# Spreading the gates of a product-key layer: one product moved from VectorE to GpSimd, masks and casts in another layout

## The chip, the core and the metric

The kernel runs on one core of a Trainium2 chip. The core has five engines with their own instruction streams: TensorE (PE in the rows; PEld is its weight load), VectorE (DVE), ScalarE (ACT), GpSimd (POOL) and SyncE (SP, which here issues DMAs only). They share the on-chip memory SBUF; TensorE writes to PSUM. Engines wait for one another through semaphores. The metric is the device time of one execution in microseconds (us); less is better.

## What is computed

One step of a one-layer encoder over 1024 prompt frames and 64 frames of a running stream: a normalised projection, band attention and retention side by side, and then PEER, a retrieval over 128 x 128 single-neuron experts. Only PEER matters here:

```
s = einsum('thcd,hckd->thck', qry, sub_keys)         # 8 heads, 2 halves, 128 keys each
top_s, top_i = top_k(s, 16)                          # per half
cand_s = top_s[..., 0, :, None] + top_s[..., 1, None, :]
cand_i = top_i[..., 0, :, None] * 128 + top_i[..., 1, None, :]
best_s, best_pos = top_k(cand_s, 16)                 # 16 of the 256 pairs
expert = take_along_axis(cand_i, best_pos)
gate = softmax(best_s)
a = einsum('td,thkd->thk', h, expert_u[expert])
y = einsum('thk,thkd->td', gelu(a) * gate, expert_v[expert])
```

A token so has 8 x 16 = 128 slots, each with a first place i and a second place j (both 0 to 127) and a gate. For 640 of the tokens the kernel does not gather rows but multiplies by all 16384 experts, with a gate matrix G[i, j] per token that is zero but at the chosen pairs. Building this matrix is the job of the spread stage:

G[i, j] = sum over slots s of (i == place_i[s]) * (j == place_j[s]) * gate[s]

## The kernel before

The program is a row of stages with a barrier of all engines behind each: `project`, `mix` (attention and retention, out projection), `route` (the two top-k searches), `spread`, `experts`. A stage is a block in which each engine has its own function; the order on an engine is the order in which its function is written, and nothing else sets it.

`spread` takes 5 tiles of 128 tokens (`NTD`), each in 16 steps of `B` = 8 tokens: 80 steps. The 128 slots lie on the 128 partitions. In a step

- VectorE (L1616) forms `hot_j`: for each of the 8 tokens a row of 128 places that is 1 where the place is the slot's j. Its layout is [slot, token, place], so its second operand, the slot's j, is constant along the innermost axis (a broadcast with step 0).
- VectorE (L1620) forms `hot_i` likewise for i, but in the layout [slot, place, token]: innermost are the 8 tokens, whose i values lie side by side, and the broadcast is over the middle axis.
- VectorE (L1625) multiplies `hot_j` by the gate (again a broadcast along the innermost axis): `cols`, in f32.
- ScalarE (L1658) casts `hot_i` to f32 `rows` and turns it to [slot, token, place] on the way, reading every eighth element.
- TensorE (L1641) multiplies, for each of the 8 tokens, `rows` (128 x 128) by `cols` (128 x 128) into PSUM `gp`; a multiplication has two entries in the trace, so a step has 16.
- ScalarE (L1662) copies `gp` into the tile's matrix `g`, turned to [i, j, token]. It does so one step late: cast of step q, then copy of step q - 1. At the end of a tile it makes the last copy before the next tile's first cast.

`hot_i`, `hot_j`, `rows` and `cols` have two buffers each, `gp` has four. The waits are: `hot_i` of a step needs the cast of two steps earlier; `cols` and the cast need the multiplication of two steps earlier; the multiplication needs both `rows` and `cols`. In the trace `g` is called `spr_g` for even tiles and `pass_g` for odd ones. A tile's matrix is stored by SyncE with one DMA, the last one in four pieces by ScalarE (L1674), and the `experts` stage starts on these.

The rows ahead of the spread stage come from other stages: `mix` uses GpSimd for squares (L585), rotary products (L602, L603, L605) and the product with a decay that is constant along the innermost axis (L615); `route` uses it for a product of bf16 tiles (L1183); `experts` for the low halves of weights (L1799). VectorE's neighbours there are L757 and L763 (two scalings of queries and keys), and L1391 in `route`.

## Time and profile before

| | us |
|---|---|
| median of 3 runs | 3593.18 (3587.45 to 3594.58) |
| time of the profiled execution | 3587.85 |
| its span in the trace | 3586.1 |
| spread stage: first VectorE step to the issue of the last stores | 1465.35 to 1710.62 |
| VectorE busy between 1465 and 1711 us | 230.45 |
| ScalarE busy there | 230.00 |
| TensorE busy there | 170.54 |
| GpSimd busy there | 0.00 |

Times in the rows are counted from the start of the span. A timeline row is "start, duration, engine, line, operation, output<-inputs, shapes, x count", and in brackets the idle time of the engine before it with what ended it. A row with x2 or more is several instructions put together, and its duration runs from the first start to the last end. Instructions of one engine may overlap by a tenth of a microsecond: the next starts while the former drains, so the spacing of starts, not the duration, is what a step costs. The engine "PEq" in a bracket is TensorE's queue, here the barrier between two stages.

### The profile page before, as it was taken

The page shows a single profiled execution, that of the slowest core. Times are in us where ns is not written, and L with a number is a line of the kernel's source. Part 1 is how long each engine was busy: PE and PEld are TensorE (multiplying, and loading weights), DVE is VectorE, ACT ScalarE, POOL GpSimd, SP SyncE. Part 2 cuts the span into 40 slices and gives each one's busy share as a digit, 9 for nine tenths or more (in the row PEclk, how much of TensorE's full clock was granted, in tenths as well). Part 3 has the DMA queues.
Part 4 walks back from the last instruction along what each step waited for, and adds up shares of the span by engine and source line. Part 5 has one row for each costly group of instructions (what it writes and reads, how often), then busy time and mean ns, then how long its engine had stood idle before and what let it go on. Part 6 is the DMA issues. An engine that isn't in the chain of part 4 may idle for free.

```text
span 3586.1 us, 51512 instructions
## 1 busy us (share of the span) xinstructions
PE 3311.0 (92%) x18470; PEld 2838.7 (79%) x18470; DVE 2502.0 (70%) x5310; ACT 1080.2 (30%) x1689; POOL 1762.7 (49%) x1341
## 2 busy tenths in 40 slices
PE   8999996999988997477799999999999999999999
PEld 6888885566656997466698998998888888888887
DVE  3111103434332999899388999999999899999998
ACT  3111112334331221699322222222222222222221
POOL 0000004332300365000477887888887788788786
PEclk9999997999999999799899999999999999999999
DMA  4222215222232000157899999999999899999998
GB/s 174 100 91 99 99 61 201 81 96 91 95 126 84 16 22 15 36 167 226 268 335 334 376 365 353 375 358 359 385 372 350 330 359 363 352 365 355 366 372 303
DMA packets 338482, 831.47 MB, mean 232 GB/s; under 512 B 25904, under 2 KB 132784, under 8 KB 336048
## 3 DMA queue, kind: packets, MB, share of 16 engines
q0 software_dynamic: 129024, 469.82, 34.9%
q1 hardware_dynamic: 165456, 314.88, 25.0%
q10 hardware_dynamic: 43872, 45.29, 3.7%
q8 instruction: 51, 0.84, 0.1%
q14 instruction: 79, 0.65, 0.1%
HBM read 741.09 MB, written 88.80 MB: 231 GB/s over the span
## 4 chain that ended last, share of the span: by engine, by line
PE 35%; DVE 11%; issue 2%; POOL 2%; DMA 2%; ACT 0%; DVEq 0%; ACTq 0%
PE exp_up L2055 17%; PE exp_vp L2072 17%; DVE exp_now L2001 6%; DMA pass_g<-in_u_rows,pass_g 2%; DVE pass_g L1972 1%; DVE exp_ring L1994 1%; DVE pass_g L1994 1%; DVE exp_up L1958 1%; POOL exp_v_lo L1804 1%; POOL exp_u_lo L1799 1%; POOL pass_g L1813 1%; DVE exp_am_lo L1963 0%; POOL exp_ring L1813 0%; DMA exp_ring<-in_u_rows,pass_g 0%; DVE exp_now L1997 0%
## 5 line engine op out<-in xcount | busy, mean ns | idle before, releaser
L2055 PE MATMUL exp_up<-dense_h_hi,exp_u_hi 128*128 128x320 f32 x2048 | 647.5, 316 | 54.6 <-DVE exp_am_lo L1963 30.1
L2055 PE MATMUL exp_up<-dense_h_lo,exp_u_hi 128*128 128x320 f32 x2048 | 634.2, 310 | 0.0
L2055 PE MATMUL exp_up<-dense_h_hi,exp_u_lo 128*128 128x320 f32 x2048 | 632.5, 309 | 0.0
L1972 DVE TENSOR_TENSOR pass_g<-pass_g,exp_vp 128x512 f32<-128x512 f32 x640 | 436.3, 682 | 129.7 <-PE exp_vp L2072 128.4
L2072 PE MATMUL exp_vp<-exp_v_hi,exp_am_hi 128*128 128x512 f32 x1280 | 504.9, 394 | 0.1
L2072 PE MATMUL exp_vp<-exp_v_hi,exp_am_lo 128*128 128x512 f32 x1280 | 503.7, 393 | 0.0
L2072 PE MATMUL exp_vp<-exp_v_lo,exp_am_hi 128*128 128x512 f32 x1280 | 502.0, 392 | 0.0
L2055 PEld LDWEIGHTS exp_up<-dense_h_hi,exp_u_hi 128*128 128x128 f32 x2048 | 385.9, 188 | 99.4 <-DVE exp_am_lo L1963 43.6
L1799 POOL TENSOR_TENSOR exp_u_lo<-pass_g,exp_u_hi 128x1024 fp32r<-128x1024 f32 x128 | 308.8, 2413 | 274.7 <-ACT exp_u_hi L1859 272.4
L2055 PEld LDWEIGHTS exp_up<-dense_h_lo,exp_u_hi 128*128 128x128 f32 x2048 | 385.5, 188 | 24.4
L2055 PEld LDWEIGHTS exp_up<-dense_h_hi,exp_u_lo 128*128 128x128 f32 x2048 | 386.1, 189 | 0.0
L1868 ACT ACTIVATE exp_up<-exp_up 128x320 f32<-128x320 f32 x256 | 108.0, 422 | 710.2 <-PE exp_up L2055 705.3
L1804 POOL TENSOR_TENSOR exp_v_lo<-pass_g,exp_v_hi 128x1024 fp32r<-128x1024 f32 x128 | 308.7, 2412 | 20.8 <-ACT exp_v_hi L1864 18.5
L340 PE MATMUL prj_zp<-prj_w_hi,prj_hT_hi 128*128 128x512 f32 x792 | 308.8, 390 | 0.0
L340 PE MATMUL prj_zp<-prj_w_lo,prj_hT_hi 128*128 128x512 f32 x792 | 308.3, 389 | 0.0
L1873 ACT CAST exp_am_hi<-exp_up 128x320 fp32r<-128x320 f32 x256 | 109.2, 426 | 640.9 <-DVE exp_up L1958 640.9
L2001 DVE SCALAR_TENSOR_TENSOR exp_now<-exp_ring,pass_g,exp_now 128x1024 f32<-128x1024 f32 x224 | 287.6, 1284 | 8.7 <-DVE exp_now L2001 0.5
L2001 DVE SCALAR_TENSOR_TENSOR exp_now<-pass_g,exp_now 128x1024 f32<-128x1024 f32 x220 | 282.5, 1284 | 9.0
L2072 PEld LDWEIGHTS exp_vp<-exp_v_lo,exp_am_hi 128*128 128x128 f32 x1280 | 241.4, 189 | 55.3
L340 PE MATMUL prj_zp<-prj_w_hi,prj_hT_lo 128*128 128x512 f32 x704 | 274.1, 389 | 0.0
L1994 DVE CUSTOM_DVE_ANT_0 pass_g<-exp_now,pass_g 128x1024 f32<-128x1024 f32 x224 | 268.6, 1219 | 6.2 <-DMA pass_g<-in_u_rows,pass_g 6.0
L1994 DVE CUSTOM_DVE_ANT_0 exp_ring<-exp_now,exp_ring 128x1024 f32<-128x1024 f32 x224 | 268.5, 1219 | 3.4 <-DMA exp_ring<-in_u_rows,pass_g 3.2
(216 smaller groups left out, 6058.1 us busy)
## 6 DMA issues: line engine op xcount, KB each, us to landing
pass_g<-in_u SPq DMA_DIRECT2D x128, 512.0 KB, 8.4
pass_g<-in_v SPq DMA_DIRECT2D x128, 512.0 KB, 6.6
pass_g<-scratch_gates SPq DMA_DIRECT2D x128, 320.0 KB, 6.7
scratch_z<-prj_zo ACTq DMA_DIRECT2D x33, 768.0 KB, 3.5
prj_w_raw<-in_w_in SPq DMA_DIRECT2D x44, 512.0 KB, 4.0
scratch_gates<-spr_g SPq DMA_DIRECT2D x2, 8192.0 KB, 30.4
scratch_gates<-pass_g SPq DMA_DIRECT2D x2, 8192.0 KB, 30.5
mix_zg<-scratch_z SPq DMA_DIRECT2D x9, 1024.0 KB, 5.3
```

The source lines that it names most:

```text
L340: last = nc.tensor.matmul(zp[:, bank(i), :], hT[p][:, k, i * P:(i + 1) * P], (w_hi, w_lo)[q][:, slot, k, :], start=(k == 0 and n == 0), st ...
L1799: nc.gpsimd.tensor_tensor(u[1][:, j % 2, :], u_raw[:, j % 2, :], u[0][:, j % 2, :].bitcast(F32), ALU.subtract).then_inc(u_lo_ready, 1)
L1804: nc.gpsimd.tensor_tensor(v[j // 2 % 2][1][:, j % 2, :], v_raw[:, j % 2, :], v[j // 2 % 2][0][:, j % 2, :].bitcast(F32), ALU.subtract).the ...
L1813: nc.gpsimd.indirect_dma_start(out=row(n), out_offset=None, in_=d["u_rows"] if n < PICKS else d["v"], in_offset=bass.IndirectOffsetOnAxis( ...
L1868: nc.scalar.activation(up[:, g, 0:GW], up[:, g, 0:GW], ACT.Gelu).then_inc(gelu_ready, 1)
L1873: nc.scalar.copy(am[0][:, half, o, cols(g)], up[:, g, 0:GW]).then_inc(am_hi_ready, 1)
L1958: V.tensor_tensor(up[:, g, 0:GW], up[:, g, 0:GW], gt[:, j % 2, cols(g)], ALU.mult).then_inc(prod_ready, 1)
L1972: V.tensor_tensor(acc[:, t, c], acc[:, t, c], vp[:, n % 4, :], ALU.add).then_inc(added, 1)
L1994: V.tensor_tensor_reduce(out=row(n), in0=now[:, :], in1=row(n), scale=1.0, scalar=0.0, op0=ALU.mult, op1=ALU.add, accum_out=dot[:, c:c + 1 ...
L2001: V.scalar_tensor_tensor(out=now[:, :], in0=row(n), scalar=dot[:, c:c + 1], in1=now[:, :], op0=ALU.mult, op1=ALU.add).then_inc(taken, 1)
L2055: last = nc.tensor.matmul(up[:, g, 0:GW], u[a][:, o, k * P:(k + 1) * P], h2[b][:, k, cols(g)], start=(k == 0 and n == 0), stop=(k == KD - ...
L2072: last = nc.tensor.matmul(vp[:, bank, :], am[b][:, 1 - half, o, t * P:t * P + P], v[1 - half][a][:, o, c], start=(o == 0 and n == 0), stop ...
```

## The change

The product with the gate moves from VectorE to GpSimd, which ran only an `iota` in this stage. Both masks get the layout [slot, token, place] and share one table `iotas`, so the table `places_j` and its cast fall away. VectorE now makes `hot_i` first, then `hot_j`; `hot_j` waits for the product of two steps earlier (`cols_ready`, which GpSimd raises by 2 at the start). ScalarE casts `hot_i` without turning it.

```diff
-        iotas = s.sb("iotas", [P, P, B], BF16)
-        hot_i = s.sb("hot_i", [P, 2, P, B], BF16)
-        places_j = s.sb("places_j", [P, B, P], BF16)
+        iotas = s.sb("iotas", [P, B, P], BF16)
+        hot_i = s.sb("hot_i", [P, 2, B, P], BF16)
...
         def _(pool):
...
+            pool.sem_inc(cols_ready, FREE)
+            pool.wait_ge(rt_in, 16)
+
+            def body(t, slot, pair, n):
+                for q, step in steps(t, n):
+                    pool.wait_ge(hot_j_ready, step + 1)
+                    pool.wait_ge(spread_ready, step + 1)
+                    nc.gpsimd.tensor_tensor(cols[:, q % 2, :, :], hot_j[:, q % 2, :, :],
+                                            rt[:, 2, at(t * P + q * B, B)].rearrange("p (b o) -> p b o", o=1).broadcast_to([P, B, P]),
+                                            ALU.mult).then_inc(cols_ready, 1)
+
+            tiles(pool, body)
...
-                    nc.vector.tensor_tensor(hot_j[:, q % 2, :, :], places_j[:, :, :],
+                    dve.wait_ge(rows_ready, step + 1)
+                    nc.vector.tensor_tensor(hot_i[:, q % 2, :, :], iotas[:, :, :],
+                                            place[:, 0, at(tok, B)].rearrange("p (b o) -> p b o", o=1).broadcast_to([P, B, P]),
+                                            ALU.is_equal).then_inc(hot_i_ready, 1)
+                    dve.wait_ge(cols_ready, step + 1)
+                    nc.vector.tensor_tensor(hot_j[:, q % 2, :, :], iotas[:, :, :],
                                             place[:, 1, at(tok, B)].rearrange("p (b o) -> p b o", o=1).broadcast_to([P, B, P]),
                                             ALU.is_equal).then_inc(hot_j_ready, 1)
-                    dve.wait_ge(rows_ready, step + 1)
-                    nc.vector.tensor_tensor(hot_i[:, q % 2, :, :], iotas[:, :, :],
-                                            place[:, 0, at(tok, B)].rearrange("p (o b) -> p o b", o=1).broadcast_to([P, P, B]),
-                                            ALU.is_equal).then_inc(hot_i_ready, 1)
-                    dve.wait_ge(hot_j_ready, step + 1)
-                    dve.wait_ge(spread_ready, step + 1)
-                    nc.vector.tensor_tensor(cols[:, q % 2, :, :], hot_j[:, q % 2, :, :],
-                                            rt[:, 2, at(tok, B)].rearrange("p (b o) -> p b o", o=1).broadcast_to([P, B, P]),
-                                            ALU.mult).then_inc(cols_ready, 1)
...
-                    pe.wait_ge(cols_ready, step + 1)
+                    pe.wait_ge(cols_ready, step + 1 + FREE)
...
-                    nc.scalar.copy(rows[:, q % 2, :, :], hot_i[:, q % 2, :, :].rearrange("p k b -> p b k")).then_inc(rows_ready, 1)
+                    nc.scalar.copy(rows[:, q % 2, :, :], hot_i[:, q % 2, :, :]).then_inc(rows_ready, 1)
```

VectorE's queue in the middle of a tile, before; `spr_` names are the spread stage's tiles, ISA is a wait, REGISTER_ALU counts up a wait's value:

```order
L1625 ISA
L1625 TENSOR_TENSOR spr_cols<-spr_hot_j,spr_rt 128x1024
L1616 ISA
L1616 TENSOR_TENSOR spr_hot_j<-spr_places_j,spr_place 128x1024
L1619 REGISTER_ALU
L1620 ISA
L1620 TENSOR_TENSOR spr_hot_i<-spr_iotas,spr_place 128x1024
```

and with the change, at the same place:

```order
L1625 REGISTER_ALU
L1626 ISA
L1626 TENSOR_TENSOR spr_hot_i<-spr_iotas,spr_place 128x1024
L1630 ISA
L1630 TENSOR_TENSOR spr_hot_j<-spr_iotas,spr_place 128x1024
```

A step has two VectorE operations in place of three, with one wait ahead of each.

GpSimd's queue at the start of the stage, before (the rows behind the `iota` are the next stage's):

```order
L1599 IOTA spr_iota 128x128
L80 UNCONDITIONAL_BRANCH
L81 ISA
L1794 UNCONDITIONAL_BRANCH
L1799 TENSOR_TENSOR exp_u_lo<-pass_g,exp_u_hi 128x1024 x2
```

and with the change:

```order
L1598 IOTA spr_iota 128x128
L1562 UNCONDITIONAL_BRANCH
L1562 ISA
L1607 ISA
L1607 TENSOR_TENSOR spr_cols<-spr_hot_j,spr_rt 128x1024
L1605 REGISTER_ALU
L1607 ISA
L1607 TENSOR_TENSOR spr_cols<-spr_hot_j,spr_rt 128x1024
```

GpSimd gets 80 products, one a step, that stood in VectorE's queue before; all other stages keep their order on it.

## Rows read from the trace of the kernel before

**Rows 1.** Busy us by engine (instructions), granted TensorE clock, DMA: whole stage, first step.

```profile
1465.00:1711.00 246.00, 170.54 (x1280) 156.27 (x1280) 230.45 (x241) 230.00 (x160) 0.00 (x0) 0.96 0.54 158
1470.00:1472.00 2.00, 2.00 (x12) 2.00 (x11) 2.00 (x3) 1.91 (x1) 0.00 (x0) 0.50 0.00 0
```

**Rows 2.** ScalarE's cast as a group: busy us, mean ns, idle before.

```profile
L1658 ACT CAST spr_rows<-spr_hot_i 128x1024 f32<-128x1024 bf16 x80 | 167.8, 2102 | 12.7 <-DVE spr_hot_i L1620 12.7
```

**Rows 3.** Timeline of a middle stretch: start us, us, engine, line, operation.

```profile
1593.17 1.22 DVE L1625 TENSOR_TENSOR spr_cols<-spr_hot_j,spr_rt 128x1024 f32<-128x1024 bf16 x1
1593.75 2.10 ACT L1658 CAST spr_rows<-spr_hot_i 128x1024 f32<-128x1024 bf16 x1
1594.30 1.22 DVE L1616 TENSOR_TENSOR spr_hot_j<-spr_places_j,spr_place 128x1024 bf16<-128x1024 bf16 x1
1595.44 0.68 DVE L1620 TENSOR_TENSOR spr_hot_i<-spr_iotas,spr_place 128x1024 bf16<-128x1024 bf16 x1
1595.69 1.07 ACT L1662 COPY spr_g<-spr_gp 128x1024 f32<-128x1024 f32 x1
...
1595.90 2.05 PE L1641 MATMUL spr_gp<-spr_cols,spr_rows 128*128 128x128 f32 x16 [0.81 <-ACT spr_rows L1658]
1596.04 1.22 DVE L1625 TENSOR_TENSOR spr_cols<-spr_hot_j,spr_rt 128x1024 f32<-128x1024 bf16 x1
1596.60 2.11 ACT L1658 CAST spr_rows<-spr_hot_i 128x1024 f32<-128x1024 bf16 x1
```

**Rows 4.** Timeline, start of the spread stage.

```profile
1465.35 1.23 DVE L1616 TENSOR_TENSOR spr_hot_j<-spr_places_j,spr_place 128x1024 bf16<-128x1024 bf16 x1 [0.27 <-DVE spr_place L1610]
...
1469.48 5.47 PE L1641 MATMUL spr_gp<-spr_cols,spr_rows 128*128 128x128 f32 x32 [14.80 <-ACT spr_rows L1658]
...
1473.20 1.01 ACT L1662 COPY spr_g<-spr_gp 128x1024 f32<-128x1024 f32 x1 [1.06 <-PE spr_gp L1641]
```

**Rows 5.** Timeline, end of the spread stage and start of the next.

```profile
1710.62 13.34 ACTq L1674 DMA_DIRECT2D scratch_gates<-spr_g  x4
...
1724.86 1.99 ACT L1859 CAST exp_u_hi<-pass_g 128x1024 fp32r<-128x1024 f32 x2 [14.27 <-PEq L82]
```

**Rows 6.** Who waited for whom in the spread stage: us in total, times, longest.

```profile
DVE spr_cols L1625 <- PE spr_gp L1641: 10.2, 5, 3.2
```

**Rows 7.** Groups by form: GpSimd products and differences, one ScalarE cast.

```profile
L1799 POOL TENSOR_TENSOR exp_u_lo<-pass_g,exp_u_hi 128x1024 fp32r<-128x1024 f32 x128 | 308.8, 2413 | 274.7 <-ACT exp_u_hi L1859 272.4
...
L1864 ACT CAST exp_v_hi<-pass_g 128x1024 fp32r<-128x1024 f32 x128 | 134.9, 1054 | 1.1 <-DMA pass_g<-in_v 1.1
...
L585 POOL TENSOR_TENSOR mix_sq<-mid_late 128x1024 f32<-128x1024 f32 x9 | 17.0, 1892 | 90.9 <-PE mix_X L886 86.7 <-DMA mid_late<-scratch_z 4.2
...
L615 POOL TENSOR_TENSOR mix_rot<-mix_rot,mix_k_dec 128x512 f32<-128x512 f32 x9 | 9.5, 1058 | 8.4 <-PE mix_X L886 8.4
```

**Rows 8.** Timeline in the attention stage: VectorE and GpSimd side by side.

```profile
569.61 1.27 POOL L602 TENSOR_TENSOR mix_part<-mix_zqk,mix_cs 128x512 f32<-128x512 f32 x1
...
570.65 1.30 DVE L757 TENSOR_TENSOR mix_qk<-mid_late,mix_qk_rs 128x1024 f32<-128x1024 f32 x1
570.83 2.25 POOL L603 TENSOR_TENSOR mix_part<-mix_zqk,mix_cs 128x512 f32<-128x512 f32 x1
571.99 2.17 DVE L763 TENSOR_TENSOR mix_qk<-mix_qk,mix_g_qk 128x1024 f32<-128x1024 f32 x1
...
573.15 2.13 POOL L605 TENSOR_TENSOR mix_rot<-mix_part 128x512 f32<-128x512 f32 x1
...
575.36 1.27 POOL L602 TENSOR_TENSOR mix_part<-mix_zqk,mix_cs 128x512 f32<-128x512 f32 x1
```

**Rows 9.** One GpSimd line of the route stage: duration ns min/median/max.

```profile
L1183 POOL TENSOR_TENSOR rt_hit<-rt_hit,rt_tf x16: 3632/4092/4557, 1186.1 to 1430.0; 128x2048 bf16<-128x2048 bf16 x16
```

**Rows 10.** Timeline in the route stage: the same line and VectorE beside it.

```profile
1184.84 2.35 DVE L1391 TENSOR_TENSOR rt_hit<-rt_places,rt_ab 128x2048 bf16<-128x2048 bf16 x2
...
1186.14 8.14 POOL L1183 TENSOR_TENSOR rt_hit<-rt_hit,rt_tf 128x2048 bf16<-128x2048 bf16 x2 [68.55 <-DVE rt_hit L1391]
```

More of the change, by code:

```diff
@@ L1604, in _ @@
             dve.wait_ge(iota_set, 1)
-            nc.vector.tensor_copy(iotas[:, :, :], iota[:, :].rearrange("p (k o) -> p k o", o=1).broadcast_to([P, P, B])
-                                  ).then_inc(tables, 1)
-            nc.vector.tensor_copy(places_j[:, :, :], iota[:, :].rearrange("p (o k) -> p o k", o=1).broadcast_to([P, B, P])
+            nc.vector.tensor_copy(iotas[:, :, :], iota[:, :].rearrange("p (o k) -> p o k", o=1).broadcast_to([P, B, P])
                                   ).then_inc(tables, 1)
@@ L1610, in _ @@
             nc.vector.tensor_copy(place[:, :, :], rt[:, 0:2, :]).then_inc(tables, 1)
-            dve.wait_ge(tables, 3)
+            dve.wait_ge(tables, 2)
             def body(t, slot, pair, n):
```

## The prediction

> **What bounds the kernel now.** The stages stand one behind another, so I first ask whether the spread stage as a whole is on the path. It is: the last stores are issued at 1710.62 us, and ScalarE's next work, the first cast of the experts stage, starts at 1724.86 after 14.27 us of idle time that the stage barrier ended [rows 5]. What the spread stage gains or loses by its last store moves everything behind it. The stage runs from 1465.35 us [rows 4] to 1710.62 us [rows 5], 245.3 us for 80 steps.
>
> Then I ask what sets a step. The busy times of the stage [rows 1] have two engines nearly full: VectorE 230.45 and ScalarE 230.00 of 246 us, TensorE 170.54, and GpSimd nothing. The timeline of a middle stretch [rows 3] shows both gapless. VectorE: `cols` at 1593.17, `hot_j` at 1594.30, `hot_i` at 1595.44, `cols` again at 1596.04. The spacing is 1.13, 1.14 and 0.60, a step of 2.87 us. ScalarE: cast at 1593.75, copy at 1595.69, cast again at 1596.60, a step of 2.85 us. TensorE works 2.05 us of a step and is idle for 0.81, until the cast. So a change has to relieve both engines, and this one means to. 79 steps of 2.87 are 226.7 us; VectorE's five waits for TensorE (10.2 us in all, [rows 6]), nearly all at the four tile ends, and the filling and draining of the pipeline are the rest.
>
> **The parts, taken alone.** *ScalarE.* The cast costs 2102 ns on average [rows 2]. One that reads and writes 1024 elements in order costs 1054 ns (L1864, [rows 7]). With the copy (spacing 0.91, [rows 3]) ScalarE comes down from 2.85 to about 1.05 + 0.91 = 1.96 us a step.
>
> *VectorE.* `hot_i` and `hot_j` have the same size and types, but `hot_i` takes 0.68 us and `hot_j` 1.22 [rows 3]; they differ in the innermost axis of the second operand, which is dense in the one and a broadcast in the other. `hot_i` gets `hot_j`'s form, so I give it `hot_j`'s spacing. The two masks then cost 1.13 + 1.13 = 2.26 us a step, against 2.87: the removed product saves 1.13, the new layout gives 0.53 back.
>
> *GpSimd.* Its product has a bf16 operand, a broadcast f32 operand and an f32 result; no row has that exact form. L615 is nearest, a product whose second operand is constant along the innermost axis: 1058 ns for 512 elements [rows 7]. L585, 1024 elements, has 1892 ns. A bf16 product of 2048 has a least duration of 3632 ns [rows 9]. From L615 and L585 the slope is (1892 - 1058) / 512 = 1.63 ns an element. I take 1.89 us, L585's value, since L615 extrapolates to it and half the bf16 row, 1.82, is close. The upper bound is L1799, two f32 tiles of 1024, 2.41 us; the lower bound is 1.82.
>
> The Trainium skill's page "GPSIMD Engine Reference", section 3.1, puts an elementwise operation with two inputs at about 2.6 cycles an element; by that, an estimate is 2.2 us for this product, and a step in the sum below would be 0.3 us longer. L615 and L585 do not bear it out for their forms.
>
> *One cast less* at the stage's start (`places_j`) gains nothing: VectorE then waited for the route data anyway, as it does now. No DMA moves in its queue; SyncE's stores and ScalarE's last stores only follow their tile.
>
> If nothing else happened, VectorE's 2.26 us would be the bound and the stage would shrink. That is the first rival below.
>
> **What the two engines do to each other.** In the attention stage VectorE and GpSimd work side by side, and there I read a collision [rows 8]. GpSimd's L602 runs alone at 575.36: 1.27 us. L603, the same shape, starts at 570.83 while VectorE's L757 runs, and takes 2.25. L757 ends at 570.65 + 1.30 = 571.95; L603 ends at 573.08, 1.13 us later. VectorE's L763 starts at 571.99, while L603 is under way, and takes 2.17, though a two-input operation of that size takes about 1.22; it ends at 574.16, 1.08 us behind L603's end. L605 starts at 573.15, takes 2.13 and ends at 575.28, 1.12 us behind L763's end. That reads as strict turns: each waits for the other to end and then needs slightly less than its own time. L757's second operand is a broadcast along the innermost axis, as the masks' is. For bf16 the route stage shows the same [rows 9, 10]: GpSimd's first product starts at 1186.14 while the second of two VectorE masks runs to 1184.84 + 2.35 = 1187.19, 1.05 us longer. L1183 has durations from 3632 to 4557 ns, 0.93 apart, and the row of a pair is 8.14 us from first start to last end. In all of these both of VectorE's inputs lie in SBUF.
>
> The changed stage has exactly this: both masks read two SBUF tiles (`iotas`, `place`), and GpSimd's product reads `hot_j` and `rt`. Before, GpSimd was idle there.
>
> The Trainium skill says it as a rule, page "SBUF — State Buffer", section "Who interferes with whom": a VectorE instruction with two SBUF inputs contends with a GpSimd instruction that reads SBUF, and whoever comes first holds the shared port for its whole instruction. The rows agree [rows 8] (2.25 us against 1.27). By this rule the move only lengthens the shared queue; without it the stage would end at the first rival's time.
>
> **The sum.** If the two take turns, a step costs the sum of both engines' turns. A turn behind the other engine is 1.08 for a VectorE operation of 1024 elements (L763, [rows 8]), and for GpSimd it is 0.14 under its own time (1.13 against 1.27). `hot_j` and the next `hot_i` stand back to back on VectorE, since neither needs the product under way: 1.08 + 1.13. GpSimd: 1.89 - 0.14 = 1.75. A step is 1.08 + 1.13 + 1.75 = 3.96 us. Which of them wins a turn does not change this sum.
>
> Everything else fits beside it. TensorE's step of 2.05 us fits, and even at the lower clock: the stage's first step, with a granted clock of 0.50 (1.2 of 2.4 GHz) [rows 1], lasts from 1469.48 to ScalarE's copy at 1473.20 [rows 4], 3.7 us, under 3.96. ScalarE has 1.96 of 3.96. At a tile's end multiplication, copy and next cast in a row, 2.05 + 1.0 + 1.05 = 4.1 us, replace a step of 3.96, and the two buffers take up the difference. So I count the 10.2 us of waits as gone.
>
> The stage: the first product ends 1.13 + 1.22 us (two masks) + 1.1 (the next `hot_i` ahead of it) + 1.75 = 5.2 us after the first mask's start. 79 steps of 3.96 make 312.8. The last multiplication and copy with their waits make 3.2. In all 321.2 us against 245.3: 75.9 us more. On the profiled execution's 3587.85 us that gives 3664. The median of the runs shown is 3593.18, 5.3 us above that execution, and a median of the new kernel may lie likewise; I take the middle, 3667 us, 2.1% above the median before.
>
> Range of this case: each 0.1 us of a step is 8 us. With 1.82 for the product the step is 3.89, and if a turn is 1.04 in place of 1.08 it is about 3.85: 67 us more, 3655. With handovers that cost 0.2 us more a step, 3680 to 3685.
>
> **The rivals.**
> - *No collision for these forms (not slower).* Then VectorE bounds with 2.26 us a step; the cycle of a product, its multiplication and the product two steps later needs (1.89 + 2.05 + 0.2) / 2 = 2.1 us a step and does not. The stage: 4.3 + 79 x 2.26 + 3.2, plus four tile ends at some 1.5 us, are 192 us, 53 less: 3535 to 3540. Against it stand [rows 8 to 10]. For it: no row has a mask of 1024 bf16 elements beside a mixed product. Its mechanism decides at the step of (245.3 - 8.4) / 79 = 3.0 us: if 1.0 us of the 3.96 overlaps in each step, the change is worth nothing.
> - *GpSimd's product is dearer.* If the mixed types cost what L1799 does, 2.41 us, the turn is 2.27 and the step 4.48: 117 us more, 3705 to 3710. For it: L1799 reads two tiles; against it: the gate is one value per 128 elements, as in L615.
> - *The product is made, but turns are lost as well.* If each change of sides costs a semaphore's way on top, about 0.1 us and two changes a step, 3.96 becomes 4.2: 3683. This lies between the two, inside the range.
>
> **Chances.** Turns at 3.85 to 4.2 us a step: 0.76. Dearer product, 4.2 to 4.5: 0.14. No collision or mostly none: 0.08. The rest, 0.02, is a collision that overlaps just enough to change nothing or little. The predicted time is the first case's, 3667. The range takes the first two, 3650 to 3710. Faster by over 0.2%: 0.08; within 0.2% (about what a measurement can tell from no change): 0.01; slower: 0.91.
>
> **What would show it.** The starts of `hot_i` are 3.96 us apart in mid tile. VectorE's masks have durations of two sorts, one near 1.2 and one near 2.8 us (1.75 waited, 1.08 own), with no semaphore wait named ahead of them. GpSimd's product lasts 1.9 to 2.9 us, with the waited turn in it. ScalarE's cast takes about 1.05 us and TensorE waits for `cols`, GpSimd's line, and no longer for `rows`. VectorE and GpSimd together are busy for more than the stage lasts, as waiting counts as busy. If instead masks stay at 1.22 and the product at 1.9 while they overlap, the collision is refuted and the first rival holds. A product of 2.4 us with masks that do not overlap it shows the second.

## The result, and the profile after

The changed kernel takes 3667.38 us (median of 5 runs, 3665.84 to 3674.52), the kernel before 3589.19 us beside it (median of 5, 3587.45 to 3594.58). The ratio is 1.0218, with an interval of 1.0206 to 1.023: slower by 78 us. The forecast was 3667 us.

The profiled execution of the changed kernel took 3666.2 us, its span is 3664.0. Its stage first. The rows are those of start and end of the spread stage (timeline: start us, us, engine, line, operation), as [rows 4, 5] for before:

```profile
1464.81 1.23 DVE L1626 TENSOR_TENSOR spr_hot_i<-spr_iotas,spr_place 128x1024 bf16<-128x1024 bf16 x1 [0.35 <-DVE spr_place L1619]
...
1467.37 2.68 POOL L1607 TENSOR_TENSOR spr_cols<-spr_hot_j,spr_rt 128x1024 f32<-128x1024 bf16 x1 [8.64 <-DVE spr_hot_j L1630]
...
1781.47 1.90 POOL L1607 TENSOR_TENSOR spr_cols<-spr_hot_j,spr_rt 128x1024 f32<-128x1024 bf16 x1 [1.16 <-DVE spr_hot_j L1630]
...
1786.57 13.33 ACTq L1679 DMA_DIRECT2D scratch_gates<-spr_g  x4
...
1800.81 1.99 ACT L1864 CAST exp_u_hi<-pass_g 128x1024 fp32r<-128x1024 f32 x2 [14.28 <-PEq L82]
```

The first mask starts at 1464.81 and the last stores are issued at 1786.57: 321.8 us, against 245.3 before and 321.2 in the forecast. The next stage's first cast stands 14.24 us behind the issue, exactly as before (1724.86 - 1710.62). The stage explains 76.5 us of the 78.35 between the two profiled executions.

The busy times of the stage, as [rows 1]: us, then TensorE, its weight loads, VectorE, ScalarE, GpSimd, granted clock, DMA share, GB/s:

```profile
1465.00:1788.00 323.00, 195.64 (x1280) 180.45 (x1280) 314.62 (x160) 156.57 (x160) 216.00 (x80) 0.85 0.41 121
```

VectorE and GpSimd together are "busy" for 314.62 + 216.00 = 530.6 of 323 us, so at least part of this is one of them standing still inside an instruction. TensorE (195.64) and ScalarE (156.57) have slack. The groups by form, as [rows 2] (busy us, mean ns, idle before):

```profile
L1630 DVE TENSOR_TENSOR spr_hot_j<-spr_iotas,spr_place 128x1024 bf16<-128x1024 bf16 x80 | 227.8, 2848 | 0.0
L1607 POOL TENSOR_TENSOR spr_cols<-spr_hot_j,spr_rt 128x1024 f32<-128x1024 bf16 x80 | 216.0, 2700 | 108.6 <-DVE spr_hot_j L1630 108.6
...
L1626 DVE TENSOR_TENSOR spr_hot_i<-spr_iotas,spr_place 128x1024 bf16<-128x1024 bf16 x80 | 99.0, 1237 | 2.1 <-ACT spr_rows L1663 1.8 <-DVE spr_place L1619 0.3
...
L1663 ACT CAST spr_rows<-spr_hot_i 128x1024 f32<-128x1024 bf16 x80 | 83.4, 1048 | 12.8 <-DVE spr_hot_i L1626 12.8
```

`hot_i` and `hot_j` now have the same form, the same table and the same sizes, and yet one has a mean of 1237 ns and the other 2848. A timeline from inside the third tile, as [rows 3], shows why:

```profile
1598.69 2.72 POOL L1607 TENSOR_TENSOR spr_cols<-spr_hot_j,spr_rt 128x1024 f32<-128x1024 bf16 x1 [1.26 <-DVE spr_hot_j L1630]
1599.57 2.91 DVE L1630 TENSOR_TENSOR spr_hot_j<-spr_iotas,spr_place 128x1024 bf16<-128x1024 bf16 x1
...
1602.41 1.21 DVE L1626 TENSOR_TENSOR spr_hot_i<-spr_iotas,spr_place 128x1024 bf16<-128x1024 bf16 x1
1602.66 2.72 POOL L1607 TENSOR_TENSOR spr_cols<-spr_hot_j,spr_rt 128x1024 f32<-128x1024 bf16 x1 [1.25 <-DVE spr_hot_j L1630]
...
1603.55 2.91 DVE L1630 TENSOR_TENSOR spr_hot_j<-spr_iotas,spr_place 128x1024 bf16<-128x1024 bf16 x1
...
1605.48 2.02 PE L1646 MATMUL spr_gp<-spr_cols,spr_rows 128*128 128x128 f32 x16 [1.73 <-issue]
1606.38 1.21 DVE L1626 TENSOR_TENSOR spr_hot_i<-spr_iotas,spr_place 128x1024 bf16<-128x1024 bf16 x1
```

This is one step, 3.97 us from `hot_i` (1602.41) to `hot_i` (1606.38). Read it by ends. The product of 1598.69 ends at 1601.41; `hot_j`, which started at 1599.57 while the product was under way, ends at 1602.48, 1.07 us later. The next product starts at 1602.66 while VectorE is in `hot_i` (to 1603.62); it ends at 1605.38, 1.76 us behind that. Then `hot_j` ends at 1606.46, 1.08 us behind the product. So each ends nearly its whole own time behind the other (a mask 1.07 or 1.08 of 1.21 us, the product 1.76 of 1.90): they hardly make progress side by side. The page of the profile calls the wait busy time, and names no releaser for it: `hot_j`'s idle time is 0.0.

### The profile page after: what moved, and what is told of

It reads as the page before. It is cut to its first block, busy times and chain, and to the rows that moved or that the text cites. A ratio compares the mean times of both kernels' runs of the same rounds, so it can differ in the third digit from the quotient of the medians.

```text
span 3664.0 us, 51581 instructions
## 1 busy us (share of the span) xinstructions
PE 3337.3 (91%) x18470; PEld 2864.0 (78%) x18470; DVE 2585.5 (71%) x5229; ACT 1007.6 (28%) x1689; POOL 1981.8 (54%) x1421
## 4 chain that ended last, share of the span: by engine, by line
PE 34%; DVE 11%; issue 2%; POOL 2%; DMA 1%; ACT 0%; DVEq 0%; ACTq 0%
PE exp_up L2060 17%; PE exp_vp L2077 17%; DVE exp_now L2006 6%; DVE pass_g L1977 1%; DVE exp_ring L1999 1%; DVE pass_g L1999 1%; DMA pass_g<-in_u_rows,pass_g 1%; DVE exp_up L1963 1%; POOL exp_ring L1818 1%; POOL exp_v_lo L1809 1%; POOL exp_u_lo L1804 1%; DVE exp_am_lo L1968 1%; DMA exp_ring<-in_u_rows,pass_g 0%; POOL pass_g L1818 0%; DVE exp_now L2002 0%
## 5 line engine op out<-in xcount | busy, mean ns | idle before, releaser
L1646 PE MATMUL spr_gp<-spr_cols,spr_rows 128*128 128x128 f32 x1280 | 195.6, 317 | 136.1 <-issue 106.6
L1646 PEld LDWEIGHTS spr_gp<-spr_cols,spr_rows 128*128 128x128 f32 x1280 | 180.4, 225 | 151.5 <-issue 144.4
```

The costliest lines, as they stand in the source:

```text
L1646: last = nc.tensor.matmul(gp[:, q % BANKS, b * P:(b + 1) * P], rows[:, q % 2, b, :], cols[:, q % 2, b, :], start=True, stop=True)
```

## The experiments

My theory: GpSimd's product and VectorE's masks, all of whose operands lie in SBUF, take strict turns, and a step is the sum of the turns, 1.13 + 1.08 + 1.75 us. The rivals: the new layout alone makes the kernel slow; or the waits along `hot_j`, product and multiplication set the step; or any work of GpSimd on the same buffers slows VectorE.

Experiments 1 to 4 ran on one chip, 5 to 8 on a second and 9 to 11 on a third, each group beside the kernel before on its chip (3609.09, 3636.77 and 3631.7 us). The three differ, so a time is compared within its group only. The expectations give times for the first runs, where the kernel before took 3589 us; read them as differences from that. "Stage" is always the stretch from the first mask's start to the issue of the last stores, read from a profile; the kernel before has one profile, from the first runs.

| | us per step | stage, us | against before of its group, us | ratio |
|---|---|---|---|---|
| before | 2.87 | 245.3 | | |
| changed | 3.97 | 321.8 | +78 | 1.0218 |
| 1: both masks' table in PSUM | 2.26 | 195.7 | -38.9 | 0.9897 [0.9881, 0.9914] |
| 2: layout only | 3.64 | 292.6 | +44.5 | 1.0124 [1.0107, 1.0141] |
| 3: product move only | 3.44 | 278.7 | +36.4 | 1.0099 [1.0082, 1.0116] |
| 4: GpSimd mostly writes | 2.48 | 209.2 | -29.6 | one run |
| 5: half a product | 3.12 | 253.2 | +6.7 | one run |
| 6: masks and product in one instruction | 3.63 | 294.3 | +45 | 1.0126 [1.0109, 1.0142] |
| 7: one mask's table in PSUM | 2.84 | 238.8 | -5.3 | 0.9988 [0.9979, 0.9998] |
| 8: 1 without the tile-end drain | 2.26 | 187.7 | -49.8 | 0.9863 [0.9847, 0.988] |
| 9: 8 with later loads | 2.26 | 188.0 | -40.7 | 0.9877 [0.985, 0.9904] |
| 10: 8 again | 2.26 | 188.1 | -46.3 | 0.9873 [0.9849, 0.9897] |
| 11: changed again | 3.97 | 322.3 | +82.2 | 1.0225 [1.02, 1.0251] |

### 1. The table of places in PSUM

```diff
-    BANKS = 4
+    BANKS = 2
...
-        iotas = s.sb("iotas", [P, B, P], BF16)
+        iotas = s.pb("iotas", [P, B, P])
+        s.sb("spare", [P, B, P], BF16)
```

The table becomes f32 in PSUM. `gp` gives up two of its four buffers for it, and `spare` only keeps the addresses of the tiles behind it. Instructions and order are those of the changed kernel; the multiplication now waits for the copy of two steps earlier and not of four.

> The changed kernel, with the table of places that both masks read lying in PSUM (f32) instead of SBUF, so that a mask has one SBUF input; to make room, the multiplication's results have 2 PSUM buffers in place of 4. All else is as in the changed kernel. Theory (VectorE with two SBUF inputs and GpSimd take strict turns): the turns are gone, masks last 1.22 us and the product 1.9 us side by side, VectorE's two masks set the step, 2.27 to 2.35 us, and the time is 3535 to 3550 us. Rival A (the product's own length or its chain over semaphores sets the step, not the inputs' place): the step stays 3.97 us and the time 3667 us. Rival B (both engines slow down side by side wherever the operands lie): something between, a product of 2.5 us or more.

Timeline of this kernel inside a tile:

```profile
1593.29 1.22 DVE L1627 TENSOR_TENSOR spr_hot_i<-spr_iotas,spr_place 128x1024 bf16<-128x1024 f32 x1
1593.55 1.90 POOL L1608 TENSOR_TENSOR spr_cols<-spr_hot_j,spr_rt 128x1024 f32<-128x1024 bf16 x1 [0.36 <-DVE spr_hot_j L1631]
...
1594.42 1.22 DVE L1631 TENSOR_TENSOR spr_hot_j<-spr_iotas,spr_place 128x1024 bf16<-128x1024 f32 x1
...
1595.55 1.22 DVE L1627 TENSOR_TENSOR spr_hot_i<-spr_iotas,spr_place 128x1024 bf16<-128x1024 f32 x1
```

The product starts at 1593.55, 0.26 us into `hot_i`, and overlaps both masks; each mask takes 1.22 us and the product 1.90. The step is 2.26 us, the first rival's number in the prediction, and the stage falls from 321.8 to 195.7 us. The layout, the row of waits along `hot_j`, product and multiplication, and GpSimd's work are those of the changed kernel, so none of the three rivals can account for the 1.71 us a step that went. Two more things changed with the place: the table's type and the number of `gp` buffers. Neither explains it: the turns in the attention stage are between f32 tiles in SBUF [rows 8], and experiment 7 has two `gp` buffers too, and its mask with two SBUF inputs still takes turns. The Trainium skill's page "SBUF — State Buffer", section "Who interferes with whom", ties the exclusion to a VectorE instruction with two SBUF inputs; this run agrees: with one input in PSUM it is gone, at 2.26 us a step in place of 3.97.

The kernel is faster than before by 38.9 us, at the edge of the 39 to 54 us expected, but its stage is 49.6 us shorter. Most of the rest went behind the stage. Its last stores and the next stage's first cast:

```profile
1663.69 21.02 ACTq L1680 DMA_DIRECT2D scratch_gates<-spr_g  x4
...
1685.63 1.99 ACT L1865 CAST exp_u_hi<-pass_g 128x1024 fp32r<-128x1024 f32 x2 [21.97 <-PEq L82]
```

The four issues take 21.02 us in place of 13.34 [rows 5], and the first cast stands 21.9 us behind the first issue, against 14.2: 7.7 of the missing 10.7 us are given back there, and the other 3 are not located. Experiment 9 comes back to this.

### 2. The layout alone

The changed kernel with the product back on VectorE, behind `hot_j`:

```diff
-                    nc.gpsimd.tensor_tensor(cols[:, q % 2, :, :], hot_j[:, q % 2, :, :],
...
                     nc.vector.tensor_tensor(hot_j[:, q % 2, :, :], iotas[:, :, :],
...
+                    dve.wait_ge(hot_j_ready, step + 1)
+                    dve.wait_ge(spread_ready, step + 1)
+                    nc.vector.tensor_tensor(cols[:, q % 2, :, :], hot_j[:, q % 2, :, :],
```

> Only the layout half of the change: both masks in the token-place layout, ScalarE casts in order, but the product stays on VectorE behind the two masks. Theory: no GpSimd, no turns, three VectorE operations with a spacing of 1.13 us each make a step of 3.40 us; 79 x 0.53 = 42 us more than before, less up to 10 us of waits at the tile ends: 3620 to 3631 us. Rival (the layout is what costs the 78 us, GpSimd nothing): 3667 us, a step of 3.97.

Timeline inside a tile:

```profile
1597.56 1.22 DVE L1614 TENSOR_TENSOR spr_hot_i<-spr_iotas,spr_place 128x1024 bf16<-128x1024 bf16 x1
...
1598.69 1.22 DVE L1617 TENSOR_TENSOR spr_hot_j<-spr_iotas,spr_place 128x1024 bf16<-128x1024 bf16 x1
...
1600.05 1.22 DVE L1622 TENSOR_TENSOR spr_cols<-spr_hot_j,spr_rt 128x1024 f32<-128x1024 bf16 x1
1601.20 1.22 DVE L1614 TENSOR_TENSOR spr_hot_i<-spr_iotas,spr_place 128x1024 bf16<-128x1024 bf16 x1
```

No turns: all three last 1.22 us, and `hot_i` rose from 0.68 to 1.22 as the prediction had it. But the step is 3.64 us, 0.24 more than expected, and the time is over the expectation with it (44.5 us more than before, 31 to 42 expected). The starts are 1.13, 1.36 and 1.15 us apart. The 1.36 is ahead of `cols`, which waits for the semaphore of `hot_j`, the instruction just ahead of it on its own engine; in the kernel before `hot_i` stood between the two [rows 3]. I read the extra 0.23 us as the former instruction's drain that can't be overlapped then. No run isolates it, so it stays a reading.

The rival of the layout has this much in it: the new layout without the move costs 44.5 us. It can't be why the changed kernel is slow, though, since there VectorE has two operations of 1.13, and experiment 1 has the same layout.

### 3. The move alone

The kernel before, with the product in GpSimd's loop as in the changed kernel, and the old layouts:

```diff
+                    nc.gpsimd.tensor_tensor(cols[:, q % 2, :, :], hot_j[:, q % 2, :, :],
...
+                    dve.wait_ge(cols_ready, step + 1)
                     nc.vector.tensor_tensor(hot_j[:, q % 2, :, :], places_j[:, :, :],
...
-                    nc.vector.tensor_tensor(cols[:, q % 2, :, :], hot_j[:, q % 2, :, :],
```

> Only the other half: the kernel before with the product on GpSimd; the mask of i keeps its dense layout (0.68 us) and ScalarE turns it. Theory, if the short mask also takes turns: 1.08 + 0.60 + 1.76 = 3.44 us a step, 3620 to 3635 us. If an operation with packed bf16 inputs does not take turns: 1.08 + 1.76 = 2.84, ScalarE's 2.86 sets the step, 3580 to 3592 us.

```profile
1596.14 0.68 DVE L1633 TENSOR_TENSOR spr_hot_i<-spr_iotas,spr_place 128x1024 bf16<-128x1024 bf16 x1
1596.39 2.18 POOL L1608 TENSOR_TENSOR spr_cols<-spr_hot_j,spr_rt 128x1024 f32<-128x1024 bf16 x1 [1.26 <-DVE spr_hot_j L1629]
1596.74 2.92 DVE L1629 TENSOR_TENSOR spr_hot_j<-spr_places_j,spr_place 128x1024 bf16<-128x1024 bf16 x1
...
1599.58 0.68 DVE L1633 TENSOR_TENSOR spr_hot_i<-spr_iotas,spr_place 128x1024 bf16<-128x1024 bf16 x1
```

In this timeline the fast mask, dense and bf16 in both operands (0.68 us), takes turns like the slow one. The product starts 0.25 us into it and ends at 1598.57, 1.75 us behind its end (1596.82). `hot_j` ends at 1599.66, 1.09 us behind the product. The step is 0.60 + 1.08 + 1.75 = 3.43 us by the turns, 3.44 measured. ScalarE's step of 2.85 isn't the bound any more. The move alone already costs 36.4 us.

### 4. GpSimd mostly writes

GpSimd multiplies one token of eight and writes zeros for the other seven, so 7/8 of the gate matrices are left out. It ran once.

```diff
-                    nc.gpsimd.tensor_tensor(cols[:, q % 2, :, :], hot_j[:, q % 2, :, :],
+                    nc.gpsimd.tensor_tensor(cols[:, q % 2, 0:1, :], hot_j[:, q % 2, 0:1, :],
...
+                    nc.gpsimd.memset(cols[:, q % 2, 1:B, :], 0.0).then_inc(cleared, 1)
```

> The changed kernel, with the product made for one token of eight only, and GpSimd writing zeros for the other seven with a memset that reads nothing (so the gate matrices of 7 in 8 of these tokens are left out). Theory, if only GpSimd's reading takes turns with VectorE: the small product (about 0.3 us) takes a turn, the memset (about 0.8 us) runs beside the masks, a step of 2.4 to 2.6 us, 3545 to 3565 us. If writing takes turns as well: 2.27 + 0.3 + 0.8 = 3.3 us a step, 3610 to 3620 us.

```profile
1598.45 1.21 DVE L1627 TENSOR_TENSOR spr_hot_i<-spr_iotas,spr_place 128x1024 bf16<-128x1024 bf16 x1
...
1598.71 1.22 POOL L1607 TENSOR_TENSOR spr_cols<-spr_hot_j,spr_rt 128x128 f32<-128x128 bf16 x1 [0.47 <-DVE spr_hot_j L1631]
1599.59 1.42 DVE L1631 TENSOR_TENSOR spr_hot_j<-spr_iotas,spr_place 128x1024 bf16<-128x1024 bf16 x1
1599.87 0.84 POOL L1610 MEMSET spr_cols<- 128x896 f32 x1
...
1600.93 1.21 DVE L1627 TENSOR_TENSOR spr_hot_i<-spr_iotas,spr_place 128x1024 bf16<-128x1024 bf16 x1
```

In this timeline the small product waits for `hot_i` to end (1599.66) and ends 0.27 us later, and `hot_j` loses 0.2 us to it. The writing of 896 elements (0.84 us) runs from 1599.87 to 1600.71, all inside `hot_j`, which then ends at 1601.01: both make progress. So GpSimd's writing beside VectorE, into the same buffers, is no cost by itself, which speaks against the last rival. What takes a turn here is the instruction that also reads, and by experiment 1 only beside a mask with two SBUF inputs. The step is 2.48, 0.22 above the 2.26 of two masks: that is the small product's turn.

### 5. Half a product

The changed kernel with the product for four of eight tokens; half of the gate matrices are left out. It ran once.

```diff
-                    nc.gpsimd.tensor_tensor(cols[:, q % 2, :, :], hot_j[:, q % 2, :, :],
+                    nc.gpsimd.tensor_tensor(cols[:, q % 2, 0:B // 2, :], hot_j[:, q % 2, 0:B // 2, :],
```

> The changed kernel, with GpSimd's product made for four of the eight tokens of a step only (the other half of cols stays zero, so half of these gate matrices are left out). Nothing else moves. If the step is the sum of the turns, it falls by the removed half's own time, 512 x 1.67 ns = 0.85 us, from 3.97 to 3.11 us; the stage is 68 us shorter than the changed kernel's. If something else than the sum set the step (a fixed wait of a mask, TensorE), it stays above 3.5 us.

```profile
1590.91 1.21 DVE L1626 TENSOR_TENSOR spr_hot_i<-spr_iotas,spr_place 128x1024 bf16<-128x1024 bf16 x1
1591.16 1.86 POOL L1607 TENSOR_TENSOR spr_cols<-spr_hot_j,spr_rt 128x512 f32<-128x512 bf16 x1 [1.25 <-DVE spr_hot_j L1630]
1592.05 2.06 DVE L1630 TENSOR_TENSOR spr_hot_j<-spr_iotas,spr_place 128x1024 bf16<-128x1024 bf16 x1
...
1594.03 1.22 DVE L1626 TENSOR_TENSOR spr_hot_i<-spr_iotas,spr_place 128x1024 bf16<-128x1024 bf16 x1
```

The product of this timeline ends at 1593.02, 0.90 us behind `hot_i`'s end; `hot_j` ends 1.09 behind it. The step falls by 0.85 us, by what the product's own turn falls (1.76 to 0.90), and the stage by 68.6. A step set by latencies of semaphores or by the number of instructions wouldn't follow the product's length one to one.

### 6. No masks and no product: one instruction for each token

```diff
+                    for c in range(B):
+                        nc.vector.tensor_scalar(rows[:, q % 2, c, :], iota[:, :], rt[:, 0, at(tok + c, 1)], None, ALU.is_equal
+                                                ).then_inc(rows_ready, 1)
+                    for c in range(B):
+                        nc.vector.tensor_scalar(cols[:, q % 2, c, :], iota[:, :], rt[:, 1, at(tok + c, 1)], rt[:, 2, at(tok + c, 1)],
+                                                ALU.is_equal, ALU.mult).then_inc(cols_ready, 1)
```

VectorE compares and multiplies in one pass and writes `rows` and `cols` itself, 16 short instructions a step. GpSimd and ScalarE's cast have nothing to do.

> The kernel before without masks as tensors and without GpSimd: VectorE compares the f32 list of places with one token's place as a per-partition scalar and multiplies by its gate in the same instruction, 128 elements each; 8 instructions make rows, 8 make cols, directly in f32, and ScalarE keeps only the copy. If the spacing of such an instruction is that of the two-scalar form in the route stage with its register handling beside it, 0.13 to 0.15 us, a step is 2.1 to 2.4 us and the time 40 to 50 us under the kernel before. If each of the 16 instructions pays a register step and a wait in line, 0.2 us or more, a step is 3.2 us or more and it is slower than before.

```profile
1590.17 1.66 DVE L1612 TENSOR_SCALAR spr_rows<-spr_iota,spr_rt 128x128 f32<-128x128 f32 x8
...
1591.75 2.14 DVE L1615 TENSOR_SCALAR spr_cols<-spr_iota,spr_rt 128x128 f32<-128x128 f32 x8
...
1593.80 1.66 DVE L1612 TENSOR_SCALAR spr_rows<-spr_iota,spr_rt 128x128 f32<-128x128 f32 x8
```

In this timeline the eight `rows` take 1.58 us from start to start, 0.20 each, and the eight `cols` 2.05, 0.26 each. I had hoped for 0.13 to 0.15; the expectation's other case, 0.2 us or more and slower than before, is what came. At 3.63 us a step this way lies 45 us above the kernel before. The collision is avoided, but 16 instructions of 128 elements cost as much as experiment 2's three of 1024 (3.64), and more than the three of the kernel before (2.87), one of which is the fast mask.

### 7. One of two masks freed

```diff
+        places_j = s.pb("places_j", [P, B, P])
...
-                    nc.vector.tensor_tensor(hot_j[:, q % 2, :, :], iotas[:, :, :],
+                    nc.vector.tensor_tensor(hot_j[:, q % 2, :, :], places_j[:, :, :],
```

with two buffers of `gp`; `hot_i` keeps its table in SBUF.

> The changed kernel with the table in PSUM for the mask of j only; the mask of i keeps two SBUF inputs (2 PSUM buffers as in the run with both in PSUM). Theory of turns: only the i mask shares a queue with the product, 1.08 + 1.76 = 2.84 us a step, between 2.26 (both in PSUM) and 3.97 (none), near the kernel before's 2.87: -15 to +5 us against it. If one shared pair of inputs were enough to hold both masks up: 3.97. If turns did not depend on the inputs: 2.26.

```profile
1591.04 1.78 DVE L1629 TENSOR_TENSOR spr_hot_i<-spr_iotas,spr_place 128x1024 bf16<-128x1024 bf16 x1
...
1592.73 1.21 DVE L1633 TENSOR_TENSOR spr_hot_j<-spr_places_j,spr_place 128x1024 bf16<-128x1024 f32 x1
1593.87 1.78 DVE L1629 TENSOR_TENSOR spr_hot_i<-spr_iotas,spr_place 128x1024 bf16<-128x1024 bf16 x1
...
1595.57 1.21 DVE L1633 TENSOR_TENSOR spr_hot_j<-spr_places_j,spr_place 128x1024 bf16<-128x1024 f32 x1
```

`hot_j` with its table in PSUM lasts 1.21 us in this timeline beside the product, `hot_i` with two SBUF operands 1.78 (over the stage, 1.72 on average). By ends: `hot_i` of 1591.04 ends at 1592.82; the product that starts under it, at 1591.69, ends at 1594.56, 1.74 us later; and `hot_i` of 1593.87 ends at 1595.65, 1.09 us behind the product. `hot_j` (1592.73 to 1593.94) lies beside the same product and loses nothing. The step is 2.84, which is the turns of `hot_i` and the product, 1.08 + 1.75. The theory foretold both this step and which of the two masks would suffer. It also shows that freeing one mask is worth almost nothing against the kernel before (-5.3 us).

### 8. Experiment 1 without the tile-end drain

In experiment 1 VectorE bounds, and the tile ends (multiplication, copy, next cast in a row on ScalarE) are no longer hidden: its 195.7 us are 17 more than 79 x 2.26. At each of the four tile ends one interval between `hot_i` starts is 4.0 to 4.2 us long in place of 2.26, 7.5 us more in all; the rest is the stage's beginning and end. Here ScalarE's steps are written in one run over all tiles, so that a tile's last copy stands behind the next tile's first cast:

```diff
-                for q, step in steps(t, n):
-                    copy_rows(q, step)
-                    if q:
-                        gates_out(q - 1, step - 1)
-                gates_out(q, step)
+            for step in range(last + 1):
+                copy_rows(step)
+                if step:
+                    gates_out(step - 1)
+            gates_out(last)
```

> The run with both tables in PSUM, and ScalarE's queue written out over all 80 steps, so that the next tile's first cast stands ahead of the tile's last copy, as within a tile. Expected: the waits of some 2.4 us at each of four tile ends go, the stage falls from 195.7 to about 187 us, and the time to about 48 us under the kernel before (against 39). If the end of the stage is held by the loads and stores that meet there, less of it is seen in the time than in the stage.

Timeline around the end of the first tile, then the last stores:

```profile
1508.18 1.22 DVE L1627 TENSOR_TENSOR spr_hot_i<-spr_iotas,spr_place 128x1024 bf16<-128x1024 f32 x1
...
1510.44 1.22 DVE L1627 TENSOR_TENSOR spr_hot_i<-spr_iotas,spr_place 128x1024 bf16<-128x1024 f32 x1
...
1512.70 1.22 DVE L1627 TENSOR_TENSOR spr_hot_i<-spr_iotas,spr_place 128x1024 bf16<-128x1024 f32 x1
...
1653.71 21.17 ACTq L1679 DMA_DIRECT2D scratch_gates<-spr_g  x4
```

The masks keep their spacing of 2.26 us across the tile's end, and the stage is 8.0 us shorter than in experiment 1. The time is 49.8 us under the kernel before: the stage's 57.6 less the 7.9 us that the store issues now take longer. This kernel beats both.

### 9. The next stage's loads moved behind

What stretches the last issues from 13.3 to 21 us? In the kernel before SyncE begins to issue the next stage's loads, with those of u, at 1692.73, 18 us ahead of the last stores; in the changed kernel 29 us ahead; in experiment 1, 7 us, and in experiment 8, 5 us. They follow the store of the fourth tile, which takes about 30 us, and a tile now takes 36. I supposed that the loads stand in the way of the stores, and held those of v, of the sums and of the picks until ScalarE is done; the two loads of u stay where they were:

```diff
+            sp.wait_ge(g_out, NTD * (P // B) + BANKS)
```

> The run with both tables in PSUM and no drain at the tile ends, with one wait more on SyncE: the loads of v, of the sums and of the picks for the next stage are issued only when the last step's copy is done (the loads of u stay where they are). In the run without it they are issued 5 us ahead of the last stores, and ScalarE's four store issues take 21.2 us where they take 13.3 in the kernel before and in the changed kernel. If the loads ahead of the stores in the DMA engines are the cause, the four issues fall back towards 13 us and the time falls by up to 8 us (0.2%), less what the later loads delay in the next stage. If the issues stay at 21 us, the cause is another, and the time is the same or worse.

The loads of u, those of v and the four stores, from its timeline:

```profile
1651.64 0.83 SPq L1590 DMA_DIRECT2D pass_g<-in_u  x2
...
1656.59 0.80 SPq L1593 DMA_DIRECT2D pass_g<-in_v  x2
1656.60 22.95 ACTq L1680 DMA_DIRECT2D scratch_gates<-spr_g  x4
```

The loads of v and what follows them are issued with the stores and not ahead of them, those of u still 5 us ahead, and the stores take 22.95 us. They didn't fall back towards 13 us. It shows only that holding these loads back this far doesn't help; the DMA share between 1655 and 1700 us is 1.00 in this trace, so the loads may still compete.

All the traces together speak for that. Where the loads of u are issued 14 us or more ahead of the stores (the kernel before, the changed one, experiments 2, 3, 5, 6, 7 and 11), the four issues take 13.3 us; at 9.5 us ahead (experiment 4) they take 16.9, and at 5 to 7 us (experiments 1, 8, 9 and 10) 21.0 to 23.0. So the stores are stretched where the loads have too little time to run ahead of them, and moving the loads behind, as here, goes the wrong way if they compete. No run takes the loads away, so what the 8 us are made of stays open. Its time, 3590.97 us (3582.69 to 3600.9), isn't better than that of experiment 10.

### 10 and 11. Both ends again

Experiment 10 is the kernel of experiment 8, experiment 11 the changed kernel, both beside 9 on one chip.

> The run with both tables in PSUM and no drain again, on the same chip as the one with late loads: 1.3 to 1.4% under the kernel before, and ScalarE's last four store issues at 21 us.

> The changed kernel again, on the same chip as these: about 78 us over the kernel before, a step of 3.97 us.

The steps are 2.26 and 3.97 us, the times -46.3 (1.27% under the kernel before) and +82.2 us, and the four issues of experiment 10 take 21.3 us. Steps are the same to a hundredth on different chips; the times against before differ from the first ones by 3.5 and 4 us.

## Why the prediction was right, point by point

**The stage is on the path.** Right. 14.24 us lie between last issue and first cast in both kernels, and for the changed kernel and experiments 2, 3, 6 and 7 the time moved by the stage's difference within 6 us. It is not the whole truth: in experiments 1, 4, 8, 9 and 10 the shorter stage runs into longer store issues.

**The parts alone.** The cast: 1048 ns, forecast 1.05. `hot_i` in the new form: 1212 ns in the median, forecast 1.22. The product unhindered: 1.90 us at 1781.47, forecast 1.89, so the dearer product (2.41, from two tiles) is out. The Trainium skill's page "GPSIMD Engine Reference", section 3.1, gave an estimate of 2.2 us; the measured 1.90 decides.

**The turns.** The row of the attention stage [rows 8] gave 1.08 for VectorE behind GpSimd, and the trace of after has 1.07 and 1.08. For GpSimd behind VectorE I took 1.75, its own time less 0.14, from a product of half the size; the trace has 1.76 and 1.77. The step came out at 3.97 against 3.96. The first 1.13 of the sum, the spacing of two masks on VectorE, is 1.14 (1602.41 to 1603.55). Experiments 1, 5 and 7 show the mechanism from three sides, and the first rival's 2.26 is what one gets when the mechanism is taken away. As made, the change collides in practically every step: the median product lasts 2.72 us.

**The ends of the stage.** The first product ends at 1470.05, 5.24 us after the first mask's start (5.2), and the tail behind the last product is 3.2 us (3.2). 5.24 + 79 x 3.97 + 3.2 are 322 us, 321.8 measured.

**What I counted as free.** Nearly right. At a tile's end, in the timeline of the first one, TensorE and GpSimd read:

```profile
1529.71 3.76 PE L1646 MATMUL spr_gp<-spr_cols,spr_rows 128*128 128x128 f32 x16 [1.08 <-issue]
...
1530.88 2.70 POOL L1607 TENSOR_TENSOR spr_cols<-spr_hot_j,spr_rt 128x1024 f32<-128x1024 bf16 x1 [1.27 <-DVE spr_hot_j L1630]
...
1534.84 1.90 POOL L1607 TENSOR_TENSOR spr_cols<-spr_hot_j,spr_rt 128x1024 f32<-128x1024 bf16 x1 [1.25 <-DVE spr_hot_j L1630]
...
1539.13 2.72 POOL L1607 TENSOR_TENSOR spr_cols<-spr_hot_j,spr_rt 128x1024 f32<-128x1024 bf16 x1 [2.39 <-DVE spr_hot_j L1630]
```

The multiplication of 1529.71 took 3.76 us at a granted clock of 0.50 and fits under the step. Here the chain was sized wrongly: I had put multiplication, copy and next cast at 4.1 us with 2.05 for the first, and it took 5.8. The products start at 1530.88, 1534.84 and 1539.13: one interval of 4.29 in place of 3.97. The fourth tile's end has one of 4.19, the second and third have none beyond 0.02: 0.5 us in all, below what the sum resolves. When the product of 1534.84 starts, VectorE is waiting for ScalarE's late cast, so nobody is ahead of it and it lasts 1.90. VectorE waits for ScalarE for 1.8 us in the whole stage, where it waited 10.2 for TensorE [rows 6]. The granted clock of the stage is 0.85 (0.96 before), and TensorE now idles for some 1.9 us in every step where it idled for 0.8; 3.76 us at the lower level of the clock are still under 3.97, so inside a tile it costs nothing.

**What the profile would show.** The two sorts of masks (1.21 and 2.91 us), the product between 1.90 and 2.72, and the absent releaser are there. One sign was named wrongly. I wrote that TensorE would wait for `cols`; the waits of the stage (us in total, times, longest) say

```profile
PE spr_gp L1646 <- issue: 106.6, 69, 2.0
...
PE spr_gp L1646 <- POOL spr_cols L1607: 18.6, 2, 16.7
```

"issue" for 69 of its idle stretches, 106.6 us, and `cols` for two, of which one, 16.7 us, is the stage's start. The timeline settles it: the multiplication of 1605.48 starts 0.10 us behind the end of the product (1605.38). So the label hid the releaser, and the reader has to look at the end that stands just ahead.

**From execution to median.** Here the number was right by luck in part. I added some 3 us, half of the 5.3 by which the median of three lay above the profiled execution. Over five runs the median of before is only 1.3 us above it, and that of the changed kernel 1.2. The sum, 3664, was 2.2 us under the profiled execution of 3666.2, since 1.9 us came in outside the stage. The two small errors were opposite in sign.

## What to carry to other kernels

Before work is moved from VectorE to GpSimd, look in the trace for a place where both already run side by side, and read it by ends: if each ends its own time behind the other, the two are one engine for such operands, and the move adds the work instead of sharing it. A mask whose constant table can lie in PSUM is out of that queue at the same duration, at the price of PSUM space; here both masks had to be freed, since one left in turns kept almost the old time. A stage that becomes shorter meets the transfers at its end earlier, so read the issue of its last stores as well.

## What the runs showed of the hardware that I had not expected

- A mask of 1024 elements takes 1.22 us with an f32 table in PSUM, as much as with a bf16 table in SBUF (experiments 1 and 2). In time the remedy costs VectorE nothing; the table took the place of two of the four `gp` buffers.
- The mask that runs at 0.68 us takes turns with GpSimd's product just as the one of 1.22 does (experiment 3, step 3.44 us).
- GpSimd's writing of 896 elements, 0.84 us, takes no turn (experiment 4).
- A VectorE instruction that waits for the one just ahead of it starts 1.36 us behind it and not 1.13 (experiment 2).
- A comparison of 128 f32 elements with a scalar for each partition costs 0.20 us from start to start, and one with a second scalar and a multiplication 0.26 (experiment 6).
- The issue of the same four stores takes 13.3 us where the next stage's first loads were issued 14 us or more ahead of it, 16.9 at 9.5 us, and 21.0 to 23.0 at 5 to 7 us (experiment 9 has the numbers). That the loads cause it is not shown.
